# Twelve transposes in one group, operand tiles by parity: the expert loop of a hybrid encoder layer

## The chip, the cores and the metric

The kernel runs on one core of a Trainium2 chip. The metric is the device time of one execution in microseconds (us), the median of several runs.

## The reference

One layer of an encoder on 512 tokens of width 1024, float32: attention and a recurrent mixer side by side (not touched here), then a mixture of 32 experts, 4 of them for each token, then a last normalisation. The part that matters:

```python
def clamped_swiglu(hcat):
    gate, lin = hcat[:, :D_EXPERT], hcat[:, D_EXPERT:]
    gate = jnp.minimum(gate, SWIGLU_LIMIT)
    lin = jnp.clip(lin, -SWIGLU_LIMIT, SWIGLU_LIMIT)
    return (lin + 1.0) * (gate * jax.nn.sigmoid(SWIGLU_ALPHA * gate))
...
    def expert_block(args):
        xb, e = args
        hcat = xb @ w_up[e] + b_up[e]
        return clamped_swiglu(hcat) @ w_down[e] + b_down[e]

    y_buf = lax.map(expert_block, (x_buf, blk_expert)).reshape(P, D)
    contrib = g_s[:, None].astype(x2d.dtype) * y_buf[dest]
    return jax.ops.segment_sum(contrib, tok_s, num_segments=M)
```

For each expert, up to 128 tokens (rows) are gathered, multiplied by `w_up[e]` (1024 x 2048, 8 MB) and, after the activation, by `w_down[e]` (1024 x 1024, 4 MB), weighted and added to the sums.

## The kernel before

The experts are 32 blocks in a row, one for each expert, two of them in each turn of a hardware loop (their parity, `par`), the last two written out behind it. A product in float32 is made from three products of halves in float32r: rows' high part by weights' high part, low by high, high by low. The weights of a block come in 12 **slots** of 1 MB (2 transfers of 512 KB, from SyncE's queue): slots 4 to 7 hold the second half of `w_up[e]` (columns that belong to the activations' half 1), slots 8, 9, 14 and 15 `w_down[e]`, and slots 10 to 13 the first half of `w_up[e+1]`, the next block's. Slot j of a block passes through:

- `load`: waits until the raw buffer is free (6 of them, RAW; it is free when the slot six before has been split), then two transfers to `w_raw`;
- `split_hi` on ScalarE (L2173): `w_hi` = high part. It waits for the load and until TensorE has used the slot four before (RING = 4);
- `split_lo` on VectorE (L2177): `w_lo` = the rest;
- `slot_matmuls` on TensorE (L2191, L2192, L2194): 12 matmuls of 512 columns.

Each engine takes its instructions in the order in which `pe_block`, `act_block`, `dve_block` and `pool_block` write them, and waits only on semaphores. Beside the slots a block n has:

- A0 and A1, `pe_turn` (L2229): four transposes each of the block's activations (`moe_act_natural`, half 0 and 1) into bank 6. `take_hi` (ScalarE, L2234) and `take_lo` (VectorE, L2240) read the bank and make `a_hi` and `a_lo`, the operands of the down-projection. `take_lo` frees the bank.
- X0 and X1: the same for the next block's gathered rows (`moe_x_gathered`), into bank 7, one after the other, giving `x_hi` and `x_lo`, operands of slots 10 to 13 and of the next block's 4 to 7. There is one pair of `x` tiles, so X0's parts may be written only when slot 7 has read the old ones.
- the biases (L2208), the slot table of the block after next (`pe_meta`, L2221: which token stands in which row, into bank 7), the selector it needs (`dve_sel`, L2244), and `dve_rows` (L2250 to L2255), which turns the table into row numbers.
- on GpSimd the gather of the rows of block n + 2 (L2267) and the scatter that adds the block's result to the sums (L2276).
- `dve_swiglu`: part 0 the linear part (L2288), part 1 the activations (L2292), after `act_gated` (L2298) on ScalarE.

TensorE's order in a block before is: slots 4, 5, A0, slots 6, 7, X0, slot 8, X1, slots 9, 10, 11, A1, slots 12, 13, biases, slot table, slots 14, 15.

Of the kernel before, what the change touches and what calls it, by code (L numbers as in the profile page):

```python
# [16 lines left out]
P = 128  # L17
# [2032 lines left out]
EXPERT_BANKS = {"U10": 2, "U11": 3, "A0": 6, "X0": 7, "X1": 7, "D0": 4, "D1": 5, "U00": 0, "U01": 1, "A1": 6, "M": 7}  # L2050
# [6 lines left out]
def experts(nc, psum, ext, keep, hn_dram, acc_dram, bias_dram, out):  # L2057
# [10 lines left out]
    with ExitStack() as ctx:  # L2068
# [8 lines left out]
        x_hi = sb("x_hi", [P, KD, P], F32R)  # L2077
        x_lo = sb("x_lo", [P, KD, P], F32R)
# [168 lines left out]
        def dve_rows(dve, n, B, it, key):  # L2247

            dve.wait_ge(B.fill_sem(key), B.count(it, key))
            dve.tensor_copy(slot[:, :], B.tile(key)[:, 0:5]).then_inc(slotd, 1)  # L2250
# [49 lines left out]
        def pe_block(pe, n, e, B, it, par, nxt, nxt2):  # L2300
            keys = [(par, "U10"), (par, "U11")]
            for j in range(4, 8):
                slot_matmuls(pe, n, j, B, it, keys, x_hi, x_lo, 2 * (j - 4), keys if j == 7 else (), True)
                if j == 5:
                    pe.wait_ge(actd, 2 * n + 1)
                    pe_turn(pe, B, it, (par, "A0"), an, 0)
            if nxt:
                pe.wait_ge(gathered, 16 * n + 32)
                pe_turn(pe, B, it, (par, "X0"), xg, 0)
# [3 lines left out]
            if nxt:  # L2313
                pe_turn(pe, B, it, (par, "X1"), xg, 1)
            slot_matmuls(pe, n, 9, B, it, keys, a_hi, a_lo, 2)
            if nxt:
                pe.wait_ge(B.free_sem((par, "X1")), B.after(it, (par, "X1")))
                first = [(par, "U00"), (par, "U01")]
                for j in range(10, 14):
                    slot_matmuls(pe, n, j, B, it, first, x_hi, x_lo, 2 * (j - 10))  # L2320
                    if j == 11:
                        pe.wait_ge(actd, 2 * n + 2)
                        pe_turn(pe, B, it, (par, "A1"), an, 1)
                biases(pe, n + 1, B, it, par, B, it + par, 1 - par)
                if nxt2:
                    pe_meta(pe, n + 2, e + 2, B, it, (par, "M"))
# [8 lines left out]
        def act_block(act, n, B, it, par, nxt):  # L2335
# [3 lines left out]
            split_hi(act, n, 9)  # L2339
            split_hi(act, n, 10)  # L2340
            if nxt:
                take_hi(act, B, it, (par, "X0"), x_hi, 0, hi_x)
# [4 lines left out]
            if nxt:  # L2347
                take_hi(act, B, it, (par, "X1"), x_hi, 1, hi_x)
# [21 lines left out]
        def dve_block(dve, n, e, B, it, par, nxt, nxt2):  # L2370
# [3 lines left out]
            lo(9, 10)  # L2374
            if nxt:
                take_lo(dve, B, it, (par, "X0"), x_hi, x_lo, 0, hi_x, 2 * n + 3)
            dve_swiglu(dve, n, B, it, par, 1, 0)
            lo(11)
            if nxt:
                take_lo(dve, B, it, (par, "X1"), x_hi, x_lo, 1, hi_x, 2 * n + 4)  # L2380
                lo(12)
            dve_swiglu(dve, n, B, it, par, 1, 1)
            if nxt:
                dve_to_row(dve, n + 1, 1 - par, n)
                lo(13, 14)
                if nxt2:
                    dve_sel(dve, n + 2, e + 2, 0)
            take_lo(dve, B, it, (par, "A1"), a_hi, a_lo, 1, hi_a, 2 * n + 2)
            if nxt:
                lo(15, 16)  # L2390
                dve_swiglu(dve, n + 1, B, it, par, 0, 0)
                if nxt2:
                    dve_rows(dve, n + 2, B, it, (par, "M"))
# [416 lines left out]
```

## Time and profile before

| | before |
|---|---|
| median of 3 runs | 1722.17 us (1721.79 to 1722.31) |
| the profiled execution | 1721.03 us, its span 1719.3 us |
| TensorE busy | 1620.2 us, 94% of the span |
| VectorE busy | 1434.0 us, 83% |
| ScalarE busy | 1106.2 us, 64% |
| GpSimd busy | 243.8 us, 14% |
| transfers | 472.80 MB, mean 275 GB/s |

The span runs from the first to the last instruction. Matmuls are pipelined: a busy TensorE may still be held back within its busy time, so paces are read from starts. The expert blocks fill the span from about 560 us to about 1700 us.

### The profile page before, as it was taken

To read this page: it belongs to the slowest core of one execution; us is meant where nothing else is said; L and a number is where in the kernel's file an instruction comes from. 1 tells how busy PE (TensorE), PEld (TensorE's weight loads), DVE (VectorE), ACT (ScalarE), POOL (GpSimd) and SP (SyncE) were. 2 spreads that over 40 slices of the span, in tenths; PEclk is the share of its full clock that TensorE was granted. 3 is DMA by queue.
4 is the path that set the end of the run, shared out by engine and by line. 5 is a ranking of instruction groups with operands and counts; after the bars stand their busy time and mean duration, and the time that the engine had idled before them with its cause. 6 is when DMAs were issued, how large, how long until landed. Compare 5 with 4: busy or idle time off the path is not lost.

```text
span 1719.3 us, 33742 instructions
## 1 busy us (share of the span) xinstructions
PE 1620.2 (94%) x12579; PEld 1322.0 (77%) x12580; DVE 1434.0 (83%) x1555; ACT 1106.2 (64%) x1080; POOL 243.8 (14%) x200
## 2 busy tenths in 40 slices
PE   7999889889796999999999999999999999999994
PEld 6778777778675778878888878888888878878883
DVE  5585677676586899999999999999999999989995
ACT  5643525433325777777777777777777777777773
POOL 0001111010103211111211112111111112111110
PEclk9999999999896999999999999999999999999997
DMA  6232101000338999999999999999999999999994
GB/s 202 74 101 55 32 14 30 10 22 15 104 136 265 361 387 375 376 384 371 385 366 385 379 378 377 375 384 380 382 368 377 383 380 375 363 369 385 384 380 132
DMA packets 208032, 472.80 MB, mean 275 GB/s; under 512 B 18782, under 2 KB 29868, under 8 KB 207852
## 3 DMA queue, kind: packets, MB, share of 16 engines
q1 hardware_dynamic: 197579, 442.22, 69.6%
q0 software_dynamic: 9792, 27.28, 7.1%
q10 hardware_dynamic: 576, 2.10, 0.3%
q8 instruction: 64, 1.05, 0.3%
q14 instruction: 21, 0.16, 0.0%
HBM read 453.83 MB, written 26.08 MB: 279 GB/s over the span
## 4 chain that ended last, share of the span: by engine, by line
PE 56%; DMA 8%; ACT 2%; DVE 2%; issue 1%; SPq 0%; POOLq 0%; DVEq 0%; ACTq 0%
PE bank L2191 18%; PE bank L2194 17%; PE bank L2192 17%; DMA w_raw<-in_expert_w_up 6%; PE bank L2229 3%; ACT moe_w_hi L2173 2%; DVE moe_w_lo L2177 1%; PE bank L2208 0%; DMA moe_x_gathered<-hn_rows,moe_gather_rows 0%; DMA sum_rows<-moe_y,moe_scatter_rows 0%; DMA x<-sum_rows 0%; SPq L1469 0%; PE bank L2221 0%; DVE moe_x_lo L2240 0%; DVE x L2675 0%
## 5 line engine op out<-in xcount | busy, mean ns | idle before, releaser
L2177 DVE TENSOR_TENSOR moe_w_lo<-w_raw,moe_w_hi 128x2048 fp32r<-128x2048 f32 x384 | 874.3, 2290 | 81.9 <-ACT moe_w_hi L2173 77.6
L2173 ACT ACTIVATE moe_w_hi<-w_raw 128x2048 fp32r<-128x2048 f32 x384 | 736.1, 1917 | 136.8 <-PE bank L2194 104.5
L2191 PE MATMUL bank<-moe_w_hi,moe_x_hi 128*128 128x512 f32 x1024 | 407.8, 398 | 0.2 <-DVE moe_x_lo L2240 0.2
L2194 PE MATMUL bank<-moe_w_lo,moe_x_hi 128*128 128x512 f32 x1024 | 400.9, 391 | 0.0
L2192 PE MATMUL bank<-moe_w_hi,moe_x_lo 128*128 128x512 f32 x1024 | 399.8, 390 | 0.0
L2191 PEld LDWEIGHTS bank<-moe_w_hi,moe_x_hi 128*128 128x128 f32 x1024 | 192.9, 188 | 42.8 <-DVE moe_x_lo L2240 4.7
L2194 PEld LDWEIGHTS bank<-moe_w_lo,moe_x_hi 128*128 128x128 f32 x1024 | 192.8, 188 | 41.9
L2192 PEld LDWEIGHTS bank<-moe_w_hi,moe_x_lo 128*128 128x128 f32 x1024 | 193.2, 189 | 38.4
L2191 PE MATMUL bank<-moe_w_hi,moe_a_hi 128*128 128x512 f32 x512 | 208.9, 408 | 1.4 <-DVE moe_a_lo L2240 1.4
L2192 PE MATMUL bank<-moe_w_hi,moe_a_lo 128*128 128x512 f32 x512 | 200.1, 391 | 0.0
L2194 PE MATMUL bank<-moe_w_lo,moe_a_hi 128*128 128x512 f32 x512 | 199.9, 390 | 0.0
L2267 POOL DMA_INDIRECT moe_x_gathered<-hn_rows,moe_gather_rows x32 | 70.8, 2213 | 602.2 <-DVE moe_gather_rows L2255 602.2
L2194 PEld LDWEIGHTS bank<-moe_w_lo,moe_a_hi 128*128 128x128 f32 x512 | 96.2, 188 | 21.7
L2191 PEld LDWEIGHTS bank<-moe_w_hi,moe_a_hi 128*128 128x128 f32 x512 | 96.2, 188 | 19.2 <-DVE moe_a_lo L2240 1.6
L2192 PEld LDWEIGHTS bank<-moe_w_hi,moe_a_lo 128*128 128x128 f32 x512 | 96.5, 188 | 17.1
L2213 POOL COPY moe_bias_rows<-biasb 128x512 bf16 (+1 forms) x32 | 55.0, 1719 | 251.2 <-DMA sum_rows<-moe_y,moe_scatter_rows 244.5
L2234 ACT ACTIVATE moe_a_hi<-bank 128x512 fp32r<-128x512 f32 x64 | 38.4, 600 | 78.1 <-PE bank L2229 78.1
L600 PE MATMUL bank<-proj_x_hi,proj_w_hi 128*128 128x512 f32 x216 | 86.0, 398 | 2.3 <-issue 2.3
L601 PE MATMUL bank<-proj_x_lo,proj_w_hi 128*128 128x512 f32 x216 | 84.8, 393 | 0.0
L602 PE MATMUL bank<-proj_x_hi,proj_w_lo 128*128 128x512 f32 x216 | 84.7, 392 | 0.0
L288 ACT ACTIVATE proj_w_hi<-proj_w_raw 128x768 fp32r<-128x768 f32 x36 | 30.1, 844 | 68.8 <-PE bank L602 68.6
L438 DVE TENSOR_TENSOR proj_w_lo<-proj_w_raw,proj_w_hi 128x768 fp32r<-128x768 f32 x36 | 34.0, 959 | 47.2 <-ACT proj_w_hi L288 47.2
(343 smaller groups left out, 2059.9 us busy)
## 6 DMA issues: line engine op xcount, KB each, us to landing
w_raw<-in_expert_w_up SPq DMA_DIRECT2D x512, 512.0 KB, 6.9
w_raw<-in_expert_w_down SPq DMA_DIRECT2D x256, 512.0 KB
proj_w_raw<-in_w_in SPq DMA_DIRECT2D x36, 384.0 KB, 3.3
mixer_bias_table<-in_att_bias SPq DMA_DIRECT2D x16, 256.0 KB
x<-in_w_o SPq DMA_DIRECT2D x8, 512.0 KB, 6.8
sum_rows<-x SPq DMA_DIRECT2D x5, 512.0 KB, 4.5
x<-in_x ACTq DMA_DIRECT2D x4, 512.0 KB
x<-in_x SPq DMA_DIRECT2D x4, 512.0 KB, 4.1
```

The source lines that it names most:

```text
L600: pe.matmul(out, w_hi[:, s, w], x_hi[:, k, :], start=(k == 0), stop=False)
L601: pe.matmul(out, w_hi[:, s, w], x_lo[:, k, :], start=False, stop=False)
L602: ins = pe.matmul(out, w_lo[:, s, w], x_hi[:, k, :], start=False, stop=(k == KD - 1))
L2173: act.activation(w_hi[:, j % RING, :], raw[:, j % RAW, :], ACT.Copy).then_inc(hi_w[j % RING], 1)
L2177: eng.tensor_tensor(w_lo[:, j % RING, :], raw[:, j % RAW, :], w_hi[:, j % RING, :].bitcast(F32), ALU.subtract)\
L2191: pe.matmul(out, s_hi[:, k, :], w_hi[:, j % RING, w], start=first, stop=False)
L2192: pe.matmul(out, s_lo[:, k, :], w_hi[:, j % RING, w], start=False, stop=False)
L2194: ins = pe.matmul(out, s_hi[:, k, :], w_lo[:, j % RING, w], start=False, stop=ends)
L2213: pool.tensor_copy(brow[:, :], biasb[:, ds(e // GRP, 1), :].rearrange("p a s -> p (a s)")).then_inc(bias_ready, 1)
L2229: ins = pe.transpose(B.tile(key)[:, P * q:P * q + P], src[:, P * k:P * k + P], ident[:, :])
L2234: act.activation(dst[:, 4 * half:4 * half + 4, :].rearrange("p k s -> p (k s)"), B.tile(key)[:, :], ACT.Copy)\
L2267: pool.indirect_dma_start(out=xg[:, :], out_offset=None, in_=hn_dram, in_offset=bass.IndirectOffsetOnAxis(ap=from_row[:, 0:1], axis=0), bo ...
```

## The change

`x_hi` and `x_lo` exist twice, and a block writes the pair of the other parity, so the next rows' parts no longer wait for slot 7. X1 gets bank 0 instead of bank 7. TensorE turns A0, X0 and X1 behind slot 5, twelve transposes in one group, and makes the slot table directly behind the A1 turn (bank 7). ScalarE takes X0's high part ahead of slot 10's split and X1's ahead of slot 11's. VectorE takes X0's low part between the splits of slots 9 and 10, X1's behind 10, then makes the selector; the row numbers come directly behind A1's low part, with one more wait (`tod`, for the scatter rows that are read from the same tile). TensorE's order becomes: slots 4, 5, A0, X0, X1, slots 6 to 11, A1, slot table, slots 12, 13, biases, slots 14, 15. No operation is added or left out.

```diff
-EXPERT_BANKS = {"U10": 2, "U11": 3, "A0": 6, "X0": 7, "X1": 7, "D0": 4, "D1": 5, "U00": 0, "U01": 1, "A1": 6, "M": 7}
+EXPERT_BANKS = {"U10": 2, "U11": 3, "A0": 6, "X0": 7, "X1": 0, "D0": 4, "D1": 5, "U00": 0, "U01": 1, "A1": 6, "M": 7}
...
-        x_hi = sb("x_hi", [P, KD, P], F32R)
-        x_lo = sb("x_lo", [P, KD, P], F32R)
+        X_hi = [sb(f"x_hi{b}", [P, KD, P], F32R) for b in range(2)]
+        X_lo = [sb(f"x_lo{b}", [P, KD, P], F32R) for b in range(2)]
...
-        def dve_rows(dve, n, B, it, key):
+        def dve_rows(dve, n, B, it, key, after=False):
 
             dve.wait_ge(B.fill_sem(key), B.count(it, key))
+            if after:
+                dve.wait_ge(tod, 2 * n)
...
                 if j == 5:
                     pe.wait_ge(actd, 2 * n + 1)
                     pe_turn(pe, B, it, (par, "A0"), an, 0)
-            if nxt:
-                pe.wait_ge(gathered, 16 * n + 32)
-                pe_turn(pe, B, it, (par, "X0"), xg, 0)
+                    if nxt:
+                        pe.wait_ge(gathered, 16 * n + 32)
+                        for i in range(2):
+                            pe_turn(pe, B, it, (par, f"X{i}"), xg, i)
             keys = [(par, "D0"), (par, "D1")]
             pe.wait_ge(B.free_sem((par, "A0")), B.after(it, (par, "A0")))
             slot_matmuls(pe, n, 8, B, it, keys, a_hi, a_lo, 0)
-            if nxt:
-                pe_turn(pe, B, it, (par, "X1"), xg, 1)
             slot_matmuls(pe, n, 9, B, it, keys, a_hi, a_lo, 2)
             if nxt:
                 pe.wait_ge(B.free_sem((par, "X1")), B.after(it, (par, "X1")))
                 first = [(par, "U00"), (par, "U01")]
                 for j in range(10, 14):
-                    slot_matmuls(pe, n, j, B, it, first, x_hi, x_lo, 2 * (j - 10))
+                    slot_matmuls(pe, n, j, B, it, first, X_hi[1 - par], X_lo[1 - par], 2 * (j - 10))
                     if j == 11:
                         pe.wait_ge(actd, 2 * n + 2)
                         pe_turn(pe, B, it, (par, "A1"), an, 1)
+                        if nxt2:
+                            pe_meta(pe, n + 2, e + 2, B, it, (par, "M"))
                 biases(pe, n + 1, B, it, par, B, it + par, 1 - par)
-                if nxt2:
-                    pe_meta(pe, n + 2, e + 2, B, it, (par, "M"))
...
             split_hi(act, n, 9)
+            if nxt:
+                take_hi(act, B, it, (par, "X0"), X_hi[1 - par], 0, hi_x)
             split_hi(act, n, 10)
             if nxt:
-                take_hi(act, B, it, (par, "X0"), x_hi, 0, hi_x)
+                take_hi(act, B, it, (par, "X1"), X_hi[1 - par], 1, hi_x)
...
             split_hi(act, n, 11)
             if nxt:
-                take_hi(act, B, it, (par, "X1"), x_hi, 1, hi_x)
                 split_hi(act, n, 12)
...
-            lo(9, 10)
+            lo(9)
             if nxt:
-                take_lo(dve, B, it, (par, "X0"), x_hi, x_lo, 0, hi_x, 2 * n + 3)
+                take_lo(dve, B, it, (par, "X0"), X_hi[1 - par], X_lo[1 - par], 0, hi_x, 2 * n + 3)
+            lo(10)
+            if nxt:
+                take_lo(dve, B, it, (par, "X1"), X_hi[1 - par], X_lo[1 - par], 1, hi_x, 2 * n + 4)
+            if nxt2:
+                dve_sel(dve, n + 2, e + 2, 0)
             dve_swiglu(dve, n, B, it, par, 1, 0)
             lo(11)
             if nxt:
-                take_lo(dve, B, it, (par, "X1"), x_hi, x_lo, 1, hi_x, 2 * n + 4)
                 lo(12)
...
             take_lo(dve, B, it, (par, "A1"), a_hi, a_lo, 1, hi_a, 2 * n + 2)
             if nxt:
+                if nxt2:
+                    dve_rows(dve, n + 2, B, it, (par, "M"), True)
                 lo(15, 16)
                 dve_swiglu(dve, n + 1, B, it, par, 0, 0)
-                if nxt2:
-                    dve_rows(dve, n + 2, B, it, (par, "M"))
```

VectorE's order in the second block of the loop's body, from the first activations' low part to the second activations; before:

```order
L2240 TENSOR_TENSOR moe_a_lo<-bank,moe_a_hi 128x512
L2177 TENSOR_TENSOR moe_w_lo<-w_raw,moe_w_hi 128x2048 x2
L2238 REGISTER_ALU
L2240 TENSOR_TENSOR moe_x_lo<-bank,moe_x_hi 128x512
L2288 TENSOR_SCALAR moe_linear_part<-bank 128x512
L2177 TENSOR_TENSOR moe_w_lo<-w_raw,moe_w_hi 128x2048
L2238 REGISTER_ALU
L2240 TENSOR_TENSOR moe_x_lo<-bank,moe_x_hi 128x512
L2176 REGISTER_ALU
L2177 TENSOR_TENSOR moe_w_lo<-w_raw,moe_w_hi 128x2048
L2292 SCALAR_TENSOR_TENSOR moe_act_natural<-moe_gated_part,moe_linear_part 128x512
```

and in the changed kernel:

```order
L2240 TENSOR_TENSOR moe_a_lo<-bank,moe_a_hi 128x512
L2177 TENSOR_TENSOR moe_w_lo<-w_raw,moe_w_hi 128x2048
L2238 REGISTER_ALU
L2240 TENSOR_TENSOR moe_x_lo<-bank,moe_x_hi 128x512
L2177 TENSOR_TENSOR moe_w_lo<-w_raw,moe_w_hi 128x2048
L2238 REGISTER_ALU
L2240 TENSOR_TENSOR moe_x_lo<-bank,moe_x_hi 128x512
L2244 ISA
L2244 TENSOR_TENSOR moe_slot_of_token<-iota,posm 128x512
L2290 TENSOR_SCALAR moe_linear_part<-bank 128x512
L2177 TENSOR_TENSOR moe_w_lo<-w_raw,moe_w_hi 128x2048
L2176 REGISTER_ALU
```

Both X parts (`moe_x_lo`) now stand around the split of slot 10, and the selector (`moe_slot_of_token`) ahead of the linear part.

TensorE's order behind slot 11, at the second activations' turn (first block of the body), in the changed kernel:

```order
L2194 MATMUL bank<-moe_w_lo,moe_x_hi 128x512
L2323 REGISTER_ALU
L2229 MATMUL bank<-ident,moe_act_natural 128x128 x4
L2218 REGISTER_ALU
L2221 ISA
L2221 MATMUL bank<-meta,moe_slot_of_token 128x5
L2221 ISA
L2221 MATMUL bank<-meta,moe_slot_of_token 128x5
L2221 ISA
L2221 MATMUL bank<-meta,moe_slot_of_token 128x5
L2221 ISA
L2221 MATMUL bank<-meta,moe_slot_of_token 128x5
```

Before, the turn was followed by slot 12's matmuls, and the four of the slot table (L2221) stood behind the biases (L2208).

## Rows read from the trace of the kernel before

**Rows 1.** The page's bandwidth over 40 slices of 43 us.
```profile
GB/s 202 74 101 55 32 14 30 10 22 15 104 136 265 361 387 375 376 384 371 385 366 385 379 378 377 375 384 380 382 368 377 383 380 375 363 369 385 384 380 132
```

**Rows 2.** Transfer queues, 600 to 1600 us: packets, MB, share of 16 engines.
```profile
q1 hardware_dynamic: 155384, 355.58, 94.6%
q0 software_dynamic: 8064, 22.07, 9.5%
```

**Rows 3.** Waits, 600 to 1600 us: us in total, times, longest.
```profile
ACT moe_w_hi L2173 <- DMA w_raw<-in_expert_w_up: 19.0, 21, 2.8
...
PEld bank L2229 <- DVE moe_x_lo L2240: 6.3, 7, 1.9
...
PEld bank L2191 <- DVE moe_x_lo L2240: 4.2, 11, 0.6
```

**Rows 4.** Chain, 1057 to 1199 us: start, length, what.
```profile
1057.53 0.44 PE bank L2229 x4
...
1080.90 0.44 PE bank L2229 x4
...
1084.12 0.44 PE bank L2229 x4
...
1092.77 0.44 PE bank L2229 x4
...
1198.53 0.44 PE bank L2229 x4
```

**Rows 5.** Chain: the transfers that it passes through after 740 us.
```profile
746.37 13.69 DMA w_raw<-in_expert_w_up
...
994.36 13.87 DMA w_raw<-in_expert_w_up
...
1242.33 13.35 DMA w_raw<-in_expert_w_up
...
1490.12 14.71 DMA w_raw<-in_expert_w_up
```

**Rows 6.** Busy us by engine, clock, transfer share, GB/s.
```profile
1057.00:1065.00 8.00, 8.00 (x44) 6.22 (x43) 8.00 (x7) 5.78 (x4) 0.00 (x0) 1.00 1.06 390
...
1076.00:1079.00 3.00, 3.00 (x15) 2.46 (x14) 2.39 (x3) 2.57 (x3) 0.00 (x0) 1.00 1.10 257
```

**Rows 7.** Timeline by engine, 1504 to 1514 us: start, length, operation [idle before].
```profile
1504.85 1.92 ACT L2173 ACTIVATE moe_w_hi<-w_raw 128x2048 fp32r<-128x2048 f32 x1 [2.83 <-DMA w_raw<-in_expert_w_up]
...
1506.80 2.29 DVE L2177 TENSOR_TENSOR moe_w_lo<-w_raw,moe_w_hi 128x2048 fp32r<-128x2048 f32 x1 [2.46 <-ACT moe_w_hi L2173]
...
1509.75 0.66 PE L2229 MATMUL bank<-ident,moe_x_gathered 128*128 128x128 f32 x4 [1.47 <-DVE moe_x_lo L2240]
...
1513.15 0.50 PE L2191 MATMUL bank<-moe_w_hi,moe_x_hi 128*128 128x512 f32 x1
```

**Rows 8.** TensorE's timeline at the biases and the slot table.
```profile
1063.39 0.39 PE L2208 MATMUL bank<-moe_bias_rows,moe_bias_selector 24*128 24x512 bf16 x4
1063.71 0.25 PE L2221 MATMUL bank<-meta,moe_slot_of_token 128*128 x4
1063.83 0.48 PE L2191 MATMUL bank<-moe_w_hi,moe_a_hi 128*128 128x512 f32 x1
```

**Rows 9.** GpSimd's timeline at a gather, and the first gather in the chain.
```profile
1031.75 2.23 POOL L2267 DMA_INDIRECT moe_x_gathered<-hn_rows,moe_gather_rows  x1 [21.91 <-DVE moe_gather_rows L2255]
...
543.58 7.30 DMA moe_x_gathered<-hn_rows,moe_gather_rows
```

**Rows 10.** Timeline by engine at the loop's end, and a stretch's transfers.
```profile
1683.37 1.93 ACT L2173 ACTIVATE moe_w_hi<-w_raw 128x2048 fp32r<-128x2048 f32 x1 [0.88 <-ACTq L2345]
...
1687.53 0.68 DVE L2292 SCALAR_TENSOR_TENSOR moe_act_natural<-moe_gated_part,moe_linear_part 128x512 f32<-128x512 f32 x1
...
1688.47 0.60 PE L2229 MATMUL bank<-ident,moe_act_natural 128*128 128x128 f32 x4
...
1683.00:1684.00 1.00, 1.00 (x6) 0.82 (x5) 1.00 (x1) 0.64 (x1) 0.00 (x0) 1.00 0.00 0
```

More of the change, by code:

```diff
@@ L2302, in pe_block @@
             for j in range(4, 8):
-                slot_matmuls(pe, n, j, B, it, keys, x_hi, x_lo, 2 * (j - 4), keys if j == 7 else (), True)
+                slot_matmuls(pe, n, j, B, it, keys, X_hi[par], X_lo[par], 2 * (j - 4), keys if j == 7 else (), True)
                 if j == 5:
@@ L2385, in dve_block @@
                 lo(13, 14)
-                if nxt2:
-                    dve_sel(dve, n + 2, e + 2, 0)
             take_lo(dve, B, it, (par, "A1"), a_hi, a_lo, 1, hi_a, 2 * n + 2)
             if nxt:
+                if nxt2:
+                    dve_rows(dve, n + 2, B, it, (par, "M"), True)
                 lo(15, 16)
                 dve_swiglu(dve, n + 1, B, it, par, 0, 0)
-                if nxt2:
-                    dve_rows(dve, n + 2, B, it, (par, "M"))
                 lo(17)
@@ L2435, in first_pe @@
             for j in range(4):
-                slot_matmuls(pe, 0, j, pro, 0, keys, x_hi, x_lo, 2 * j)
+                slot_matmuls(pe, 0, j, pro, 0, keys, X_hi[0], X_lo[0], 2 * j)
             pe.wait_ge(bd_done, NT)
@@ L2456, in first_act @@
             for i in range(2):
-                take_hi(act, pro, 0, (0, f"X{i}"), x_hi, i, hi_x)
+                take_hi(act, pro, 0, (0, f"X{i}"), X_hi[0], i, hi_x)
             split_hi(act, 0, 3)
@@ L2495, in first_dve @@
             for i in range(2):
-                take_lo(dve, pro, 0, (0, f"X{i}"), x_hi, x_lo, i, hi_x, i + 1)
+                take_lo(dve, pro, 0, (0, f"X{i}"), X_hi[0], X_lo[0], i, hi_x, i + 1)
             dve_rows(dve, 1, pro, 0, (1, "M"))
@@ L2538, in lead_in @@
                 for j in range(4):
-                    slot_matmuls(eng, n, j, B, it, keys, x_hi, x_lo, 2 * j)
+                    slot_matmuls(eng, n, j, B, it, keys, X_hi[0], X_lo[0], 2 * j)
                 biases(eng, n, B, it, 0, B, it, 0)
@@ L2542, in lead_in @@
                 for i in range(2):
-                    take_hi(eng, B, it, (0, f"X{i}"), x_hi, i, hi_x)
+                    take_hi(eng, B, it, (0, f"X{i}"), X_hi[0], i, hi_x)
                 for j in range(7):
@@ L2551, in lead_in @@
                 for i in range(2):
-                    take_lo(eng, B, it, (0, f"X{i}"), x_hi, x_lo, i, hi_x, 2 * n + i + 1)
+                    take_lo(eng, B, it, (0, f"X{i}"), X_hi[0], X_lo[0], i, hi_x, 2 * n + i + 1)
                 for j in range(6):
```

## The prediction

> **What bounds the kernel now.** I read the page first: its bandwidth row shows the part that matters, the expert loop from slice 14 on, at 360 to 390 GB/s in all its slices but the last [rows 1]. Then I read the transfer queues over 600 to 1600 us: the weight queue (q1) takes 94.6% of the sixteen engines' time and the indexed transfers (q0) 9.5%, together 104% [rows 2]. So in this stretch there is no slice in which the transfer engines rest. Then the waits: TensorE's weight loads waited only for `moe_x_lo`, 6.3 us at the turns and 4.2 us at the matmuls that follow, and ScalarE waited 21 times for an up-projection load, 2.8 us at most [rows 3]. Last the chain in order of time, which gives two paces:
>
> TensorE's own. The second activations' turn starts at 1057.53 and, four blocks on, at 1198.53, with no wait between: 141.00 / 4 = 35.25 us a block [rows 4].
>
> The transfers'. Four times, 7 blocks apart each, the chain passes through the same load (that of slot 10), and ScalarE starts on it 0.02 us after it lands. The landings are start plus length of the rows: 746.37 + 13.69 = 760.06, 1008.23, 1255.68 and 1504.83 [rows 5]. The spacings are 248.17, 247.45 and 249.15 us, or 35.45, 35.35 and 35.59 a block, mean 744.77 / 21 = 35.47. At both ends of each spacing the engine was waiting for the transfer, 84 loads lie between, and the queues were never empty. So 35.47 is the rate at which the weights arrive. TensorE, 0.22 us faster a block, catches up about 1.5 us in 7 blocks and then stands still for as much. The `moe_x_lo` stalls are therefore not lost time of their own: they are the form in which a transfer-bound loop shows itself.
>
> A second way to the same number: a block loads 12 x 1.049 = 12.58 MB, and q1 moved 355.58 MB in 1000 us [rows 2], which makes 35.4 us. With weights alone in flight the rate was 390 GB/s, and 257 GB/s while the scatter's packets were served [rows 6]; the first alone would make 12.58 / 0.390 = 32.3 us, and gather and scatter take the remaining 3 us.
>
> **The change part by part.**
>
> Operand tiles by parity, X1 in bank 0. They remove the reason for which the next rows' turns stood apart: today the X1 turn waits until X0's low part has left bank 7, and in VectorE's order that comes after the split of load 10. In the worst block ScalarE takes the load at 1504.85, VectorE splits it from 1506.80 for 2.29 us, X0's low part follows, the turn starts at 1509.75 after 1.47 us idle, then come slot 9 and, at 1513.15, slot 10 [rows 7]. After the change slot 10 needs only the same split, until 1509.09, and X1's low part, as long as X0's (0.66 to the turn): 1509.8, or 3.4 us earlier than now. Slot 11 needs the next split, and ahead of it stand the selector and the linear part (0.7 each at most, like the activations' operation of [rows 10]): 1509.8 + 1.4 + 2.3 = 1513.5, against 1513.15 + 2.74 now, 2.4 us earlier. So TensorE may run at most some 2.4 to 3.4 us further ahead than today before it waits for `moe_w_lo` itself. That lead is taken once, not in each block, because the loads land when they did.
>
> Twelve transposes in one group. A group of four takes 0.44 us, and the slot behind a turn takes 3.22 - 0.44 = 2.78 against (8.65 - 0.44) / 3 = 2.74 for the three of the next stretch [rows 4]. Two groups fewer save 0.04 to 0.1 us a block on TensorE; bounds 0 and 0.2.
>
> The slot table's matmuls behind the A1 turn. Now they start 0.32 us after the bias matmuls and end with the next matmul 0.12 us later [rows 8]. Behind a turn no row shows them. Lower bound: 0.12 us move over and nothing else changes, net 0, or a gain of 0.05 if the 0.32 shrinks; upper bound: they add a drain like that of the biases, +0.32. I take 0.05. TensorE's own block becomes 35.25 - 0.08 + 0.05 = 35.2, bounds 35.0 and 35.6.
>
> VectorE and GpSimd. VectorE's work is the same; the selector and the slot table's three small copies move ahead. The new waits: the turn's wait for the gather stands before slots 6 to 15. The gather's indices are ready some 1.5 us behind the A1 turn's low part, about 3 us after the turn starts, where now GpSimd starts 9.5 us after it (1031.75 against a turn at 1057.53 - 35.25 = 1022.28). The X turns will start where the A0 turn ends, two slots of 2.74 ahead of today's X0 turn: 35.25 - 8.65 - 3.22 - 5.5 = 17.9 us after A1's start. With a microsecond between indices and issue, 14 us are left for an issue and landing that took 7.3 us at the loop's head [rows 9]. It is hidden, by 4 us at least even if it took 10. The wait on the slot table ahead of splits 15 and 16 is for matmuls that TensorE ended a microsecond earlier. Both cost 0.
>
> The sum. In the loop, the loads land at 35.47 a block as before: 0. At the end, the last load is in by 1683 (0 GB/s from 1683 to 1684), ScalarE takes it at 1683.37, the activations are done at 1687.53 + 0.68 = 1688.21 and the last turn starts at 1688.47 [rows 10]. With TensorE and ScalarE ahead, the load is taken on landing, 0.4 to 1 us earlier, and the turn follows at once, 0.3 earlier still. All behind it stays: 1.0 us gained, bounds 0.4 and 1.4. The profiled execution took 1721.03 us (span 1719.3), which lies 1.14 below the median of 1722.17; from the median, 1721.2.
>
> The Trainium skill gives the transfers more room than the trace does. In "DMA: Bandwidth & Descriptors", section Bandwidth, a 16 MB load on a core that runs alone reaches 425 GB/s. By that a block's 12.58 MB and q0's share would need some 31.5 us (an estimate from that page), TensorE would be the only bound, and the whole of its waits would be won. This case's trace does not show such a rate: 390 with weights alone, with the queues full.
>
> **The rivals.**
>
> *The transfers have room* (the rate rises when TensorE asks for more). For it: several blocks in a row at exactly 35.25. (The rule of the Trainium skill named above says the same.) Against it: 104% busy, and the spacings of [rows 5], which would be 7 x 35.25 if the loads kept up. All of 35.47 down to about 35.15 would be won: 31 x 0.32 = 9.9 us, 1712.3. Chance 0.12. Halfway, because the gather is served 6 us before the scatter and no longer beside it, 0.1 to 0.2 us a block: 3 to 6 us, 1716 to 1719. Chance 0.09.
>
> *Slower: the table's matmuls drain the array behind the turn.* They sit between 128-wide transposes and a 512-wide matmul. If each border costs what the bias-to-table border costs, 0.32, twice, TensorE needs 35.25 - 0.08 + 0.64 = 35.8 and sets the pace: 31 x (35.8 - 35.47) = +10, 1732. It decides from 0.3 us a block on; below that the transfers cover it. Chance 0.06.
>
> *Slower: the transfers are disturbed.* Loads are asked for up to 3 us earlier and more of them stand beside gather and scatter; 0.1 us a block is the spread of the three spacings, +3 to +4: 1725.5. Chance 0.06.
>
> *Slower: the gather lands after the activations' turn.* It decides from 14 us on, twice what [rows 9] show; a late microsecond a block would show only beyond the 0.22 of slack: +20. Chance 0.02.
>
> **How the numbers follow.** Forecast 1721.2, chance 0.65, its own range 1719.5 to 1722.8 (the bounds above, 0.3 of spread between executions, and half a microsecond for the order of scatter and loads). About 0.2%, 3.4 us, is what can be told from no change. Faster: 0.12 + 0.09 = 0.21; slower: 0.06 + 0.06 + 0.02 = 0.14; same 0.65. The range leaves out the 9.9 us case and the two dearest slow ones (0.20 together) and takes in most of the others: 1714.5 to 1725.0.
>
> **What the profile after would show.** Right: the waits for `moe_x_lo` gone, and in their place waits of TensorE for `moe_w_lo` at slots 10 and 11 and more of ScalarE for the loads (above 40 us where 21 stand now); the bandwidth and 104% unchanged; turns 35.4 to 35.5 us apart on the mean; the last load landing within half a microsecond of before. Wrong: turns 35.2 apart throughout with q1 above 358 GB/s (the first rival), or 35.6 and more with no waits for splits (the second).

## The result and the profile after

The changed kernel takes 1713.36 us (median of 6 runs, 1709.29 to 1714.22), the kernel before 1721.98 us in the same job: ratio 0.9952, 95% interval 0.9939 to 0.9965. It is 0.5% faster, below the forecast range of 1714.5 to 1725.0. A second job gave 1714.85 against 1721.69, ratio 0.9963 (0.9950 to 0.9976); that median lies just inside the range.

The page of the changed kernel, bandwidth over 40 slices, transfer queues over 600 to 1600 us, and the shares of the chain that ended last. They answer to [rows 1, 2].

```profile
GB/s 203 74 102 56 30 16 30 10 22 15 105 132 272 367 387 373 382 385 378 384 368 382 385 379 384 374 381 381 382 374 382 377 379 380 370 382 381 375 385 129
...
q1 hardware_dynamic: 155943, 356.85, 94.7%
q0 software_dynamic: 8244, 22.53, 9.5%
...
DVE 28%; DMA 26%; issue 8%; ACT 4%; SPq 2%; PE 0%; DVEq 0%; POOLq 0%; ACTq 0%
```

The same shares in the kernel before:

```profile
PE 56%; DMA 8%; ACT 2%; DVE 2%; issue 1%; SPq 0%; POOLq 0%; DVEq 0%; ACTq 0%
```

TensorE has left the chain; transfers and splits carry it. The weight queue moved 356.85 MB where it moved 355.58: 0.36% more. So small is the effect in the loop, and so small is what one has to explain.

Its waits over 600 to 1600 us (us in total, times, longest), against [rows 3]:

```profile
ACT moe_w_hi L2173 <- DMA w_raw<-in_expert_w_up: 161.2, 195, 2.8
...
ACT moe_w_hi L2173 <- DMA w_raw<-in_expert_w_down: 54.5, 81, 1.6
...
PEld bank L2191 <- DVE moe_w_lo L2177: 1.7, 3, 0.7
...
PEld bank L2191 <- DVE moe_x_lo L2240: 0.2, 1, 0.2
```

ScalarE now takes most loads the moment they land, TensorE almost never waits, and the stall on `moe_x_lo` is gone. TensorE's timeline, at the second activations' turns of blocks 3, 21, 22, 26, 30 and 31, with the slot table behind one of them and the new group of twelve (four plus eight) in between:

```profile
696.44 0.60 PE L2229 MATMUL bank<-ident,moe_act_natural 128*128 128x128 f32 x4
...
1331.88 0.60 PE L2229 MATMUL bank<-ident,moe_act_natural 128*128 128x128 f32 x4
...
1349.41 0.60 PE L2229 MATMUL bank<-ident,moe_act_natural 128*128 128x128 f32 x4
1349.85 1.04 PE L2229 MATMUL bank<-ident,moe_x_gathered 128*128 128x128 f32 x8
...
1367.10 0.60 PE L2229 MATMUL bank<-ident,moe_act_natural 128*128 128x128 f32 x4
1367.53 0.24 PE L2221 MATMUL bank<-meta,moe_slot_of_token 128*128 x4
...
1507.95 0.60 PE L2229 MATMUL bank<-ident,moe_act_natural 128*128 128x128 f32 x4
...
1649.58 0.60 PE L2229 MATMUL bank<-ident,moe_act_natural 128*128 128x128 f32 x4
...
1679.75 0.66 PE L2229 MATMUL bank<-ident,moe_act_natural 128*128 128x128 f32 x4 [1.25 <-DVE moe_act_natural L2294]
```

Two paces stand in it. From 1331.88 to 1507.95 five blocks take 35.21 us each: TensorE's own. From 696.44 to 1649.58 the 27 blocks take 953.14, or 35.30 each. The kernel before, read at the same two turns:

```profile
702.11 0.60 PE L2229 MATMUL bank<-ident,moe_act_natural 128*128 128x128 f32 x4
...
1659.71 0.60 PE L2229 MATMUL bank<-ident,moe_act_natural 128*128 128x128 f32 x4
```

That is 957.60 / 27 = 35.47. "Pace" below is always the distance of these two turns over 27.

Where the 8.4 us of span went (1719.3 to 1710.9). The first gather is issued on GpSimd at 541.21 instead of 543.58. Nothing ahead of it was changed, and in the profiles of this study it lies between 538.00 and 546.91: these 2.4 us are chance. From there to block 3's turn: 155.23 us instead of 158.53, 3.3 gained, all of it up to the first block's second activations. The first gather's rows are turned 5.71 us after its issue instead of 7.35, 1.64 sooner; in the light kernels below, before and after the change, it is 7.27 and 7.24, so this is chance too. Then the first block takes 1.58 less, because its X1 turn no longer stands still for 2.00 us. The three blocks from there to block 3 take 107.55 instead of 107.63, which is nothing. The first rows' turn before and after, and that stall of the kernel before:

```profile
550.93 1.97 PE L2229 MATMUL bank<-ident,moe_x_gathered 128*128 128x128 f32 x8 [3.47 <-DMA moe_x_gathered<-hn_rows,moe_gather_rows]
...
585.50 0.66 PE L2229 MATMUL bank<-ident,moe_x_gathered 128*128 128x128 f32 x4 [2.00 <-DVE moe_x_lo L2240]
```

```profile
546.92 1.97 PE L2229 MATMUL bank<-ident,moe_x_gathered 128*128 128x128 f32 x8 [1.83 <-DMA moe_x_gathered<-hn_rows,moe_gather_rows]
```

The 27 blocks: 4.5 gained. The last block gives 1.4 back: its turn comes 30.17 us after the one before, not 28.76 (1688.47 in [rows 10]), with 1.25 us idle, because TensorE now ends its work ahead of the last load. Together 2.37 + 3.30 + 4.46 - 1.41 = 8.72, which is the distance between the last turns of the two kernels. Of it 4.0 are chance (2.37 and 1.64) and 4.7 are the change. The profile of the second job, taken apart in the same way, gives 6.1 to the change, 5.8 of them in the 27 blocks. The medians of the two jobs differ from the kernel before by 8.6 and 6.8.

### The profile page after: what moved, and what is told of

It reads as the page before. It is cut to its first block, busy times and chain, and to the rows that moved or that the text cites. A ratio compares the mean times of both kernels' runs of the same rounds, so it can differ in the third digit from the quotient of the medians.

```text
span 1710.9 us, 33652 instructions
## 1 busy us (share of the span) xinstructions
PE 1614.8 (94%) x12579; PEld 1325.2 (77%) x12580; DVE 1421.8 (83%) x1555; ACT 1105.6 (65%) x1080; POOL 251.6 (15%) x200
## 4 chain that ended last, share of the span: by engine, by line
DVE 28%; DMA 26%; issue 8%; ACT 4%; SPq 2%; PE 0%; DVEq 0%; POOLq 0%; ACTq 0%
DMA w_raw<-in_expert_w_up 23%; DVE moe_w_lo L2177 21%; ACT moe_w_hi L2173 4%; DMA w_raw<-in_expert_w_down 2%; SPq L1469 1%; DVE moe_act_natural L2294 1%; DVE moe_a_lo L2240 1%; DVE moe_slot_of_token L2244 1%; DVE moe_linear_part L2290 1%; DVE moe_x_lo L2240 1%; DMA sum_rows<-moe_y,moe_scatter_rows 0%; DMA x<-sum_rows 0%; DMA moe_x_gathered<-hn_rows,moe_gather_rows 0%; DVE moe_slot_token L2254 0%; SPq L2613 0%
## 5 line engine op out<-in xcount | busy, mean ns | idle before, releaser
L2191 PE MATMUL bank<-moe_w_hi,moe_a_hi 128*128 128x512 f32 x512 | 203.4, 397 | 1.7 <-DVE moe_a_lo L2240 1.7
L2278 POOL DMA_INDIRECT sum_rows<-moe_y,moe_scatter_rows x32 | 82.5, 2577 | 220.2 <-ACT moe_y L2369 220.2
L2213 POOL COPY moe_bias_rows<-biasb 128x512 bf16 (+1 forms) x32 | 29.3, 916 | 249.7 <-DMA sum_rows<-moe_y,moe_scatter_rows 243.2
```

The source lines that it names most:

```text
L2191: pe.matmul(out, s_hi[:, k, :], w_hi[:, j % RING, w], start=first, stop=False)
L2278: pool.indirect_dma_start(out=acc_dram, out_offset=bass.IndirectOffsetOnAxis(ap=to_row[:, par:par + 1], axis=0), in_=y[:, :], in_offset=No ...
```

## The experiments

Seventeen runs, sixteen of them with an edit. "Light" kernels leave out eight matmuls a block (low part of the rows times high part of the weights, two slots of the linear part), each 0.23 us from start to start, so TensorE's pace is some 1.8 us a block shorter and what remains is the transfers' own pace. Each ratio is against the kernel before in the same job. The paces are each read from one profiled execution.

**The parts alone.** First the turns by parity without the table's move (the changed kernel with the edit below, and with `dve_sel` and `dve_rows` at their old places too), then the reverse: the kernel before with these three moved.

```diff
-                        if nxt2:
-                            pe_meta(pe, n + 2, e + 2, B, it, (par, "M"))
                 biases(pe, n + 1, B, it, par, B, it + par, 1 - par)
+                if nxt2:
+                    pe_meta(pe, n + 2, e + 2, B, it, (par, "M"))
```

> The changed kernel with the slot table, the selector and the row numbers back at their old places: the gather is issued late, as before, and only the operand tiles and the group of twelve turns remain. Theory A (loads that are asked for earlier keep the transfer engines fuller, so the loads land faster than 35.43 us a block): the turns alone do it, about -8 us, ratio 0.995 to 0.996. Theory B (the gather served apart from the scatter saves transfer time): the gain goes with the table, about -2 to -3 us, ratio 0.998 to 0.999. Theory of the prediction (transfers fixed): -1 us.

> The kernel before with only the slot table behind the second activations' turn, the selector ahead of the linear part and the row numbers behind the second activations' low part: the gather is issued some 6 us earlier, the turns stand apart as before. Theory A: no gain, ratio 0.999 to 1.001, because the X1 turn still waits. Theory B: -5 us or more, ratio about 0.997.

The turns alone: 1720.85, ratio 0.9989 (0.9976 to 1.0001), pace 35.47. The table alone: 1724.43, ratio 1.0013 (1.0000 to 1.0026), pace 35.55. Neither is clearly faster; together they are. The waits show what each lacks. Of the first, 600 to 1600 us:

```profile
ACT moe_w_hi L2173 <- DMA w_raw<-in_expert_w_up: 91.2, 113, 2.6
...
PEld bank L2229 <- DMA moe_x_gathered<-hn_rows,moe_gather_rows: 11.2, 18, 3.1
```

The rows' turn comes two slots earlier but the gather does not, so the gather is waited for, on top of the loads. How much that wait costs by itself no run shows, since here the gather is also still issued only some 4 us ahead of the scatter. In the second, TensorE's weight loads wait in every block:

```profile
PEld bank L2191 <- DVE moe_x_lo L2240: 9.1, 28, 0.3
```

The selector stands ahead of X1's low part on VectorE there and delays it by 0.3 us in all 28 blocks; TensorE itself becomes the bound at 35.55 (its light version, further down, is faster: 35.41). In the changed kernel X1's low part stands ahead of the selector, and is ready at 1149.12, 0.9 us before slot 10's first matmul at 1150.02:

```profile
1148.44 0.68 DVE L2240 TENSOR_TENSOR moe_x_lo<-bank,moe_x_hi 128x512 fp32r<-128x512 f32 x1
```

The earlier table also gives the gather back part of the room that the earlier turn took.

**What bounds: light kernels before and after.**

```diff
-                    pe.matmul(out, s_lo[:, k, :], w_hi[:, j % RING, w], start=False, stop=False)
+                    if j not in (12, 13):
+                        pe.matmul(out, s_lo[:, k, :], w_hi[:, j % RING, w], start=False, stop=False)
```

> The kernel before with 8 matmuls a block left out (low rows by high weights in slots 12 and 13), so TensorE's own block is 1.8 us shorter. If TensorE is the bound: 31 x 1.8 = -56 us, ratio 0.968. If the transfers are: the same time within 0.3%, and turns 35.4 us apart. Theory A expects somewhat less than 35.43, because TensorE frees the ring earlier.

> The changed kernel with the same 8 matmuls a block left out. Transfers as bound: within 2 us of the changed kernel, turns 35.2 to 35.3 apart. TensorE as bound: -56 us against the changed kernel. If it comes out at the same pace as the lightened kernel before, then the order does not change the transfers' rate, and the gain lies in how TensorE and the transfers take turns in being late.

Before, light: 1721.28, ratio 0.9988 (0.9975 to 1.0001), pace 35.41. After, light: 1715.00, ratio 0.9968 (0.9952 to 0.9983), pace 35.24. Fifty-odd microseconds of TensorE's work gone and nothing gained: the transfers bind, as forecast. But the changed kernel's transfers are 0.17 us a block faster with the same bytes. The medians bear it out: of the same job, the two kernels' mean times differ by 5.2 +- 2.7 us (95%, from the 12 and 10 executions). Nor are the transfer engines fuller after the change (theory A): the two queues' shares over 600 to 1600 us add up to 104.3% before (94.8 + 9.5) and 104.2% after (94.6 + 9.6). Turns of blocks 3, 4, 5 and 30 before, then of 3 and 30 after:

```profile
702.64 0.60 PE L2230 MATMUL bank<-ident,moe_act_natural 128*128 128x128 f32 x4
...
736.44 0.60 PE L2230 MATMUL bank<-ident,moe_act_natural 128*128 128x128 f32 x4
...
773.93 0.60 PE L2230 MATMUL bank<-ident,moe_act_natural 128*128 128x128 f32 x4
...
1658.79 0.60 PE L2230 MATMUL bank<-ident,moe_act_natural 128*128 128x128 f32 x4
```

```profile
693.70 0.61 PE L2230 MATMUL bank<-ident,moe_act_natural 128*128 128x128 f32 x4
...
1645.29 0.60 PE L2230 MATMUL bank<-ident,moe_act_natural 128*128 128x128 f32 x4
```

The light kernel before does not run evenly: 33.80 us from block 3 to block 4, 37.49 to block 5, and so on to the end. Over an odd number of blocks such a pace depends on which kind stands at the ends. From block 4 to block 30, 26 blocks, it is 922.35 / 26 = 35.47, the full kernel's own pace, and 35.23 in the changed one; so the transfers gained 0.17 to 0.25 us.

**The changed kernel again.** No edit.

> The changed kernel once more, in five rounds, since its first profile took 8.4 us off the span of which the thirty-two blocks themselves gave 4.6 (35.30 us a block against 35.47). Theory A (the change saves 0.17 us a block because both the bound of the transfers and that of TensorE move, and the rest of the 8.6 us of the first comparison is chance in the phases ahead of the experts): 5 to 7 us, a ratio of 0.996 to 0.997, and again turns 35.3 apart. Theory C (something ahead of the experts is faster too, by the shorter queue on GpSimd or otherwise): 8 us or more, 0.995 or less, as before.

1714.85, ratio 0.9963 (0.9950 to 0.9976), pace 35.25. The interval holds both theories' ends; the pace speaks for the loop.

**Gather and scatter apart, in the other order.** One wait more for the scatter, on top of the turns alone:

```diff
             for k in ("D0", "D1"):
                 pool.wait_ge(B.free_sem((par, k)), B.after(it, (par, k)))
+            if B is main and not last:
+                pool.wait_ge(hi_a, 2 * n + 3)
```

> The turns by parity alone (the first experiment, gather at its old place beside the scatter), with one wait more in the GpSimd queue: a block's scatter starts only when the next block's first activations are turned and copied, some 13 us after its gather. So the two indexed transfers are apart, but in the other order, and the gather is as late as before. Theory B (gather and scatter cost the weight loads more when they are served beside each other): the loads' pace falls from 35.45 to about 35.3 us a block and the time to 1716 to 1718, a ratio of 0.9965 to 0.998. Theory A1 (what helps is that the gather is asked for early, at a time when the loads have slack, and apartness is nothing): 35.45 as in the first experiment, ratio 0.999. A third way is that the late scatter holds the copy of the next y back: then ScalarE waits on GpSimd before the copies of y and the time goes over 1724.

> The kernel with the late gather and the still later scatter (turns by parity alone, scatter 13 us after the gather), without the eight matmuls a block (low part of the rows times high part of the weights, third and fourth slot of the linear part), so that TensorE lies 1.8 us below the loads and the pace is that of the transfers. Theory B (what counts is that gather and scatter are not served beside each other, in whichever order): 35.20 to 35.30 us a block between turns, as in the light kernel with the early gather (35.24 to 35.27), ratio 0.996 to 0.9975. Theory A1 (the early asking counts): 35.45, as where the two stand beside each other, ratio 0.9988.

The full kernel: 1719.21, ratio 0.9984 (0.9974 to 0.9994), pace 35.33, between the two theories' figures and nearer to B's; the gather was waited for here too (8.3 us over 13 waits). But the profiled execution was the fastest of eleven (1715.26), and by the ratios this kernel can't be told from the turns alone. Its light version: 1717.08, ratio 0.9976 (0.9955 to 0.9996), which tells nothing of either theory, because in its trace the bound is the gather:

```profile
PEld bank L2230 <- DMA moe_x_gathered<-hn_rows,moe_gather_rows: 61.4, 28, 3.6
```

All 28 blocks wait, pace 35.94. This trace is no typical one either: its execution took 1734.35, the ten others 1710.86 to 1722.49, and what bound those no trace shows. The row numbers stand behind weight splits on VectorE, and with TensorE shortened they come too late for the early turn.

**The gather held back beside the scatter.**

```diff
             if nxt2:
+                for k in ("D0", "D1"):
+                    pool.wait_ge(B.free_sem((par, k)), B.after(it, (par, k)))
                 pool_gather(pool, B, it, (par, "M"))
```

> The changed kernel without the eight matmuls a block, with one wait more: the gather, whose row numbers are ready early, is held on GpSimd until the copies of y are done, so it is asked for directly ahead of the scatter. Nothing else is changed beside the light kernel with the early gather. Theory B (beside each other they cost the loads 0.2 us a block more) and theory A1 (the early asking counts) both say 35.41 to 35.47 us a block instead of 35.24 to 35.27, ratio 0.9985 to 0.999. If the pace stays at 35.27, neither the time of the gather nor its neighbour is the cause, and the table's or the selector's new place would be.

1907.64, ratio 1.1126 (1.1066 to 1.1186), a miss by all theories. TensorE waits 152.6 us in 24 blocks for the gather, up to 9.3 us each, and the pace is 41.56:

```profile
PEld bank L2230 <- DMA moe_x_gathered<-hn_rows,moe_gather_rows: 152.6, 24, 9.3
```

It tells nothing of the loads' tariff, but much of the margin: the turn that was moved two slots ahead depends on the gather's early place.

**The same question in the old order of turns,** where the gather has room. The table alone, light; the late scatter alone, light; both, light (same edits as above).

> The kernel before with only the table, the selector and the row numbers at their new, earlier places (the second experiment), and without the eight matmuls a block, so that TensorE no longer sets its pace. The gather is then asked for some 8 us ahead of the scatter, not 2.6 us as in the light kernel before (35.41 us a block). Theory B (gather and scatter served beside each other cost the loads more) and A1 (the early asking): 35.25 us a block, as in the light changed kernel, ratio 0.996 to 0.998. If it stays at 35.4, the earlier gather alone doesn't speed the transfers and the light changed kernel's 35.25 needs another cause, in the turns.

> The light kernel before (without the eight matmuls a block), with the scatter held back until the next block's first activations are turned and copied. Gather and scatter are apart, the gather is as late as before, and here the turn of the rows comes 12 us behind the gather, so it isn't waited for. Theory B: 35.25 us a block, ratio 0.996 to 0.998. Theory A1: 35.41 as in the light kernel before, ratio 0.9988. The copies of y of the next block come 20 us later and shouldn't wait for it.

> The light kernel in the old order of turns with the table early (35.41 us a block) and with the scatter held back to the next block's first activations. Gather and scatter were some 8 us apart there already and now are about 16. Theory B2 (in the old order the early gather was still being served when the scatter started, so they were not apart after all): 35.24 to 35.32. Theory S (what counts is where in the block the scatter stands, not its distance from the gather): the same, 35.32, as with the late scatter and the late gather. If it stays at 35.41, the early gather takes back what the late scatter gives.

Table alone: 1719.36, ratio 0.9977 (0.9958 to 0.9995), pace 35.41. Late scatter alone: 1714.67, ratio 0.9959 (0.9942 to 0.9976), pace 35.32. Both: 1714.11, ratio 0.9957 (0.9940 to 0.9974), pace 35.30. GpSimd's timeline at one gather and scatter of the kernel before, and of the changed kernel, shows what "apart" means:

```profile
1066.97 2.26 POOL L2267 DMA_INDIRECT moe_x_gathered<-hn_rows,moe_gather_rows  x1 [19.00 <-DVE moe_gather_rows L2255]
1071.18 1.58 POOL L2276 DMA_INDIRECT sum_rows<-moe_y,moe_scatter_rows  x1 [1.95 <-ACT moe_y L2367]
```

```profile
1126.42 2.25 POOL L2269 DMA_INDIRECT moe_x_gathered<-hn_rows,moe_gather_rows  x1 [16.29 <-DVE moe_gather_rows L2257]
1134.15 2.83 POOL L2278 DMA_INDIRECT sum_rows<-moe_y,moe_scatter_rows  x1 [5.48 <-ACT moe_y L2369]
```

4.2 us before, 7.7 after, and in the light kernels at the like place 2.6 (before), 7.7 (after), 8.4 (table alone), 7.5 (late scatter), 14.2 (both). The late scatter works although the gather is as late as ever, so the early asking (A1) is not it. In the same job its mean time is 4.4 +- 2.6 us below that of the table alone.

The table alone, 8.4 us apart, seems to gain nothing: 35.41 as in the light kernel before. But it too runs unevenly (36.06 us from block 3 to block 4, then 33.86), and this time long blocks stand at both ends of the 27. Turns of blocks 4 and 30:

```profile
740.58 0.60 PE L2230 MATMUL bank<-ident,moe_act_natural 128*128 128x128 f32 x4
...
1660.53 0.60 PE L2230 MATMUL bank<-ident,moe_act_natural 128*128 128x128 f32 x4
```

That is 919.95 / 26 = 35.38, against 35.47 for the light kernel before, 35.31 for the late scatter, 35.29 for both and 35.23 for the changed kernel, all over the same 26 blocks. So the early gather alone gains a part of what the others do, and its ratio, 0.9977, lies below 1 as well.

**No gather at all,** at three places of the scatter: in the changed kernel, in the kernel before, and in the changed kernel with the late scatter, all light. The experts' rows are never fetched; the blocks compute on zeros.

```diff
-            pool.indirect_dma_start(out=xg[:, :], out_offset=None, in_=hn_dram,
-                                    in_offset=bass.IndirectOffsetOnAxis(ap=from_row[:, 0:1], axis=0),
-                                    bounds_check=T - 1, oob_is_err=False).then_inc(gathered, 16)
+            pool.sem_inc(gathered, 16)
```

> The changed kernel with the eight matmuls a block left out (as in the fourth experiment, so TensorE is about 1.8 us a block below the loads and the pace is that of the transfers) and with no gather at all: the experts' rows are never fetched, all blocks compute on zeros. It measures what a gather costs the loads. Theory A and B alike put an early gather at about 1.2 us a block (so 34.05 us a block beside 35.24, some 1676 to 1680 in all, ratio 0.973 to 0.976). If the gather's rows only fill gaps of the loads, the pace stays near 35.2 and the time near 1714. Between the two lies an answer to how much placing can be worth at most: the measured cost is the ceiling.

> The light kernel before without any gather (the blocks compute on zeros): the scatter alone, at its old place and in the old order of turns. The same without gather in the new order of turns took 34.26 us a block. Theory B (gather and scatter beside each other are what costs): 34.26 here too, so 1.15 less than the light kernel before, against 0.98 in the new order. Theory S or T (the place of the scatter, or the order of turns): 34.4 or more, 1.0 less than with the gather.

> The light changed kernel without any gather, its scatter held back to the next block's first activations. Theory S (the scatter costs the loads less at that place, whatever stands beside it): 34.1 to 34.2 us a block instead of 34.26. Theory B (there is no gather to be apart from): 34.26, unchanged.

1682.74 (ratio 0.9774, 0.9759 to 0.9789), 1681.20 (0.9781, 0.9720 to 0.9841) and 1679.03 (0.9768, 0.9714 to 0.9822); paces 34.26, 34.28 and 34.27. Turns of blocks 3 and 30 of the one in the old order:

```profile
691.99 0.60 PE L2230 MATMUL bank<-ident,moe_act_natural 128*128 128x128 f32 x4
...
1617.54 0.60 PE L2230 MATMUL bank<-ident,moe_act_natural 128*128 128x128 f32 x4
```

Without a gather neither the order of turns nor the scatter's place matters. What the change saved on the transfers is therefore part of the gather's price, which is not fixed: 35.41 - 34.28 = 1.13 us a block beside the scatter, 35.24 - 34.26 = 0.98 in the changed kernel, 35.32 - 34.28 = 1.04 and 35.30 - 34.28 = 1.02 with the late scatter, and 1.13 for the table alone. Over 26 blocks, which is the better reading of the uneven two, it is 1.20 beside the scatter and 1.10 for the table alone; the others move by 0.01 at most.

**Rows without a token left out of the scatter,** in the changed kernel, in its light version, and in the kernel before. They are added to rows that nobody reads.

```diff
-                                    in_=y[:, :], in_offset=None, bounds_check=T + P - 1, oob_is_err=True,
+                                    in_=y[:, :], in_offset=None, bounds_check=T - 1, oob_is_err=False,
```

> The changed kernel with a scatter that leaves out the rows of a block that hold no token (they are added to rows of the table that nobody reads). It is a try for a faster version and a test of the bound. If the transfers still bound the changed kernel at all, the fewer rows move the pace from 35.30 us a block to TensorE's own 35.2, 2 to 3 us in all, 1710 to 1712 beside 1713 to 1715 of the changed kernel in the same job, and ScalarE's waits for loads shrink below 100 us. If TensorE alone bounds it, the time is the same within 0.1% while those waits shrink all the same. If skipped rows cost the queue as much as moved ones, neither changes.

> The changed kernel with the scatter that leaves out rows without a token, and without the eight matmuls a block: it shows the transfers' own pace behind the fastest kernel so far, which TensorE bounds at 35.21 in every block. The pace there is 35.24 to 35.27 with all the rows moved; the scatter writes some 30% fewer bytes in the software queue. Theory D (a row's cost goes with its bytes): 34.7 to 34.9 us a block. Theory E (the cost is the packets' or the queue's own, little of it the bytes): 35.1 to 35.2.

> The kernel before, whose scatter leaves out the rows of a block that hold no token, and nothing else. If the transfers bind it and a left-out row costs less than a moved one, the pace falls from 35.47 to TensorE's own 35.25 us a block (its floor in the kernel before), 6 us in all, ratio 0.9955 to 0.997, and the stalls of the first activations' low part shrink. If TensorE had been the bound, nothing changes (ratio 1.000 within 0.001). It also says how much of the changed kernel's gain was to be had without the change.

In the changed kernel: 1710.48, ratio 0.9926 (0.9910 to 0.9941), while the changed kernel in the same job had 0.9963 (0.9950 to 0.9976). The intervals are apart: this version beats both kernels. Light: 1711.67, ratio 0.9945 (0.9926 to 0.9963), pace 35.05. In the kernel before: 1716.16, ratio 0.9974 (0.9959 to 0.9988), pace 35.34, TensorE's own 35.25 in most blocks. Turns of blocks 3 and 30 and waits of the first:

```profile
697.63 0.60 PE L2229 MATMUL bank<-ident,moe_act_natural 128*128 128x128 f32 x4
...
1648.63 0.60 PE L2229 MATMUL bank<-ident,moe_act_natural 128*128 128x128 f32 x4
```

```profile
ACT moe_w_hi L2173 <- DMA w_raw<-in_expert_w_up: 76.9, 88, 2.6
ACT moe_w_hi L2173 <- PE bank L2194: 71.8, 102, 0.9
```

951.00 / 27 = 35.22: TensorE's own pace in all 27 blocks, and ScalarE waits for TensorE's slots again as well as for loads. Here the bound has moved, since the light version shows 0.17 us of slack below it.

## Why the prediction was wrong

*What bounds the kernel now* held. The light kernel before shows a transfer-bound loop, and the stalls on `moe_x_lo` were its form: they vanished and most of the time stayed. That ScalarE would wait more than 40 us for loads was right (161.2 + 54.5).

*"In the loop, the loads land at 35.47 a block as before: 0"* is the step that failed. The loop gained 0.17 to 0.22 us a block. I had measured 35.47 well (the two turns give the same), and then treated it as a constant of the weights' bytes, though the text itself said that 3 us of it are gather and scatter at a lower rate. A transfer-bound stage whose cost includes two indexed transfers has no fixed pace when one of them is moved; the term should have been some 0.2 us a block, not 0. The halfway rival said so (0.1 to 0.2, 1716 to 1719), with a chance of 0.09. Its size is the measured one, at its upper end, and its chance was far too small: that the gather would be issued well ahead of the scatter was certain by the order of the program. Its reason, that gather and scatter are no longer served beside each other, is borne out in part: without a gather the gain is gone, and a late scatter gives most of it; but the distance does not order the prices (see the end of this section). Of the 3 us that the prediction gave to gather and scatter the gather has 1.0 to 1.2; the scatter's share was not measured.

*The transfers have room*, the 9.9 us rival, is not what happened: the transfers' own pace fell to 35.24, and TensorE's 35.21 is reached in stretches only. Its time of 1712.3 is near the first median by luck: 4.0 us of the first profile's gain are chance at the first gather. The rate with weights alone can be higher than my 390 GB/s: 408 in this row of the changed kernel's windows (stretch, its length, busy time of each engine, clock, transfer share, GB/s), and 408 in the kernel before from 1086 to 1089, so the change did not raise it. It is lower than the 425 GB/s of the Trainium skill, "DMA: Bandwidth & Descriptors", section Bandwidth; no run here shows that figure.

```profile
1110.00:1113.00 3.00, 3.00 (x15) 2.49 (x14) 2.22 (x2) 2.69 (x3) 0.13 (x1) 1.00 1.06 408
```

*TensorE's own block, 35.25 - 0.08 + 0.05 = 35.2*: 35.21 measured. The turns alone have four blocks in a row at 35.11 to 35.17, one of them below (844.75 to 879.90), so the group gave about 0.1 and the table took about 0.06. The drain rival did not occur here. The sum would have been good for a TensorE-bound loop, and it now matters: 35.21 is the floor that the fastest version sits on.

```profile
844.75 0.60 PE L2229 MATMUL bank<-ident,moe_act_natural 128*128 128x128 f32 x4
...
879.90 0.60 PE L2229 MATMUL bank<-ident,moe_act_natural 128*128 128x128 f32 x4
```

*The gather is hidden "by 4 us at least"*: it is not waited for in the loop of the changed kernel, but the room was overrated. Of the 14 us between issue and turn there are 11.8 (issued at 1126.42, turned at 1138.21), because the issue comes 6.3 us behind the A1 turn (1120.15) and not 4; and issue to landing takes 8.7 us under load (median, against 7.30 at the loop's head). That leaves 3 us, and the turns alone, without the table's move, waited.

*The slot table and the new waits cost 0*: right in this combination, 0.3 us a block in the old order of turns (e2). My bound of +0.32 held it for another reason than the one I gave: not a drain, but VectorE's queue.

*The end, 1.0 us gained*: ScalarE takes the last load at 1674.85 after 1.53 us idle, and the turn follows 4.90 us later, against 5.10 before: 0.2 gained there. The loop's head, of which the sum says nothing, gave 3.3: 1.6 by chance, 1.6 because the first block's X1 turn no longer stood still.

*The signs.* The waits for `moe_x_lo` went as forecast, but TensorE's waits for `moe_w_lo`, said to take their place, are three, 1.7 us in all. The mean distance of the turns, 35.30, lies outside the 35.4 to 35.5, and ScalarE takes the last load 8.5 us earlier (1674.85 against 1683.37), where the landing was to move by half a microsecond.

What stays open: why the table alone in the old order, with the two 8.4 us apart, saved less (1.10 us is left of the gather's price) than the late scatter at 7.5 us did (1.03), or the changed kernel at 7.7 (0.98). Distance at issue is then not the whole rule for the gather's price, and why the price depends on the place at all was not shown. The execution times tell the light kernel before from the changed one, and the table alone from the late scatter, within their jobs; the smaller steps rest on paces, each of one profiled execution. The changed kernel's two profiles differ by 0.05 us a block, so such steps are not certain.

## What to carry to other kernels

In a transfer-bound stage ask what makes up its pace, and price each part that the change moves: shorten the compute (a light kernel) to read the transfers' own pace, and drop one transfer to read its share. Where blocks come in pairs, read a pace over an even number of them. Two moves that are each worth nothing alone can be worth 0.4% together, when each opens the room that the other needs, so test the parts alone before calling one idle. And look at what is transferred for nobody: leaving out dead rows of the scatter was one line, and with the change it brought the loop down to TensorE's own pace.

## What the hardware showed unexpectedly

Left-out rows are not free. In the light changed kernel q0 fell from 22.66 MB to 15.23 MB in 1000 us, a third, with as many packets:

```profile
q1 hardware_dynamic: 156024, 356.87, 94.6%
q0 software_dynamic: 8269, 22.66, 9.6%
```

```profile
q1 hardware_dynamic: 157469, 359.82, 96.6%
q0 software_dynamic: 8352, 15.23, 5.9%
```

Per block that is 0.80 - 0.53 = 0.27 MB less, which at 400 GB/s would be 0.67 us (an estimate; 400 lies near the stretches with weights alone); the pace fell by 35.24 - 35.05 = 0.19, from one profile each. The software queue's share of time fell by 3.7 points, but the weight queue's rose by 2.0 only. The gather, 0.28 MB a block by the same count (22.66 MB against 15.21 MB without it, in the kernel with the late scatter), costs 0.98 us or more. So an indexed transfer's price here is not that of its bytes: dropping bytes by index gave back less than a third of their time, dropping the whole transfer more than all of it.
